# Unread products ahead of ten transpositions of probabilities, and the fourth tile's search rounds at every second unit

## The chip, the cores and the metric

The kernel runs on one core of a Trainium2 chip. The metric is the device time of one execution in microseconds (us). Five engines work side by side, each through its own queue of instructions in order, and wait for one another at semaphores: TensorE (PE in the profile; PEld are its weight loads), VectorE (DVE), ScalarE (ACT), GpSimd (POOL) and SyncE (SP), which only issues transfers.

## The reference, cut to what matters

One transformer layer on 512 rows of width 1024, all in float32. Only the attention part is touched by the change.

```
h = rms_norm(x); proj = h @ w_in              # columns for group A, its indexer, and group B
# group A (8 heads): per query the indexer's score picks 128 keys
score = sum_h relu(qi_h . ki) * wi_h;  idx = top_k(score, 128)
y_a   = softmax(q . k[idx]) @ v[idx]
# group B (4 heads): two maps per head
y_b   = rms_norm((softmax(q1 . k1) - lam * softmax(q2 . k2)) @ v)
x = x + concat(y_a, y_b) @ w_o
x = x + moe(rms_norm(x))                      # 4 of 32 experts per row, dense weights of all 32 read
```

Queries and keys mix causally in chunks of 64 rows.

## The kernel before, in words

The 512 rows are four tiles `t` of 128. The kernel has three parts: the input projection, attention with the output projection and the router, and the experts. The experts' part (`gate_up` and `down`, from about 360 us) streams 384 pieces of weights of 1 MB and splits each into an upper and a lower half.

Up to the experts, the order of all engines is one list, `PLAN`, written by `make_plan` (lines 117 to 218). Each engine walks through the same list and does its own share of each entry, so the list is the order in each engine's queue. Attention is cut into 64 units, numbered by `unit(n)`: a unit is one map of one query tile (`t`, `j`). `j` from 0 to 7 are the eight maps of group B's four heads, `j` from 8 to 15 the eight heads of group A. Units 16 to 23 are group B of tile 0, 24 to 31 group B of tile 1, 32 to 47 tile 2 (B, then A), 48 to 63 tile 3 (B, then A). The function `attend(n)` appends the work of one step, called step n here:

- `score` n: three products into one of two score banks of PSUM (L1704, the mask's product L1706 or L1710, L1711), then the row maximum on VectorE (`nmax`, L1343), then the exponential on ScalarE (L1034).
- `combine`: for group B, after each second unit, VectorE adds the two maps of a head (L1351, L1352, L1355).
- `w_hi` and `w_lo`, in steps 24 to 29 only: a piece of the output weights is rounded by ScalarE (L956) and its remainder taken by VectorE (L552).
- `next_search`: one search round (`topk`) of the indexer's scores. A round finds a row's eight largest values and marks them (MAX8 L1331; value load and MATCH_REPLACE8 L1332). 16 rounds make a tile's mask. Tile 3's rounds 0 and 1 stand in steps 22 and 23, the others from step 32 on.
- `turn_p`: the probabilities of unit n - 2 (group B: of the head that ended with it) are transposed on TensorE (L1651) into one of two transposition banks, `TP_BANK` and the bank after it, and evacuated by ScalarE (L1044).
- `values`: the transposed probabilities of one unit earlier times the values (L1740).
- `LATE`: what stands in a table for step n, among it `mix_b` and `mix_scale` (group B's norm), `turn_y` (transposition of the mixed heads, with a split by L1076 and L1388 or L1391), `out_proj` t k (one of eight parts of tile t's output projection, six products of 512 columns, L1644 to L1646), `post` (x + projection, L1448, and its square on ScalarE, L1095), `turn_x1`, `post_norm` (L1460) and `route` (the router, L1772, and eight small VectorE instructions from L1472 to L1482).

At the start of step 16 t + 7, ahead of its score (step 55 for tile 3), a loop appends all rounds that are left and then `mask` t (L1336), which writes the mask of group A's scores of tile t. The product that adds it in the first such unit (`j` = 8, unit 56 for tile 3) waits for it on TensorE:

```
if t >= 1 and n in (8, 16 * t + 7):
    while search and search[0][1] <= t:
        plan.append(search.pop(0))
    plan.append(("mask", t))
```

`last_unit(pr)` is the number of the last unit of a product `pr` of probabilities and values. `wait_bank` waits until the transposition that used the bank before has been read.

Of the kernel before, what the change touches and what calls it, by code (L numbers as in the profile page):

```python
# [28 lines left out]
P = 128  # L29
SEQ, D = 512, 1024  # L30
T = SEQ // P
# [49 lines left out]
def unit(n):  # L81

    if n < 16:
        return n // 8, 8 + n % 8
    if n < 32:
        return (n - 16) // 8, n % 8
    return n // 16, n % 16
# [6 lines left out]
def product_of(n):  # L94

    if not 0 <= n < UNITS:
        return None
    t, j = unit(n)
    if j < 8:
        return ("B", t, j // 2) if j % 2 else None  # L100
    return ("A", t, j - 8)
# [15 lines left out]
def make_plan():  # L117

    pieces = list(range(4 * (WO + 2)))
    plan = []  # L120
    for k in range(0, KD, 2):
        m = pieces.pop(0)
        plan += [("turn_h", k), ("turn_h", k + 1), ("w_hi", m), ("w_lo", m)]
    plan += [("setup",)]
    scores = [("iscore", t, h) for t in range(1, T) for h in range(HI)]
    search = [("topk", t, r) for t in range(1, T) for r in range(ROUNDS_TOPK)]

    def next_search(n):
        for _ in range(n):
            if search and ("iscore", search[0][1], HI - 1) in plan:  # L130
                plan.append(search.pop(0))

    def lower():

        split = [st[1] for st in plan if st[0] == "w_lo"]
        ready = [st[1] for st in plan if st[0] == "w_hi" and st[1] not in split]
        if plan[-1][0] == "w_hi":
            ready = ready[:-1]
        plan.extend(("w_lo", m) for m in ready[:1])

    def attend(n):
        if n == UNITS + 5:
            plan.append(("biases",))
        if n < UNITS:
            t, j = unit(n)
# [4 lines that stand above are left out]
            plan.append(("score", n))  # L150
        if product_of(n - 1) and product_of(n - 1)[0] == "B":
            plan.append(("combine", product_of(n - 1)))
        if n >= 24:
            if pieces:
                plan.append(("w_hi", pieces.pop(0)))
            lower()
        if n >= 32:
            next_search(1)
        if product_of(n - 2):
            plan.append(("turn_p", product_of(n - 2)))  # L160
        if product_of(n - 3):
            plan.append(("values", product_of(n - 3)))
        plan.extend(LATE.get(n, []))

    attended = list(range(max(LATE) + 1))
    n_items = len(ITEMS)
    first_kv = ITEM_NO[(CH["kvi"], 0)]
    for s in range(n_items + 3):

        def back(d, keep=lambda name: name != "bv"):  # L170

            u = s - d
            return [u] if 0 <= u < n_items and keep(CHUNKS[ITEMS[u][0]][0]) else []

        def all_of(kind, us):
            for u in us:
                plan.append((kind, u))

        def not_bk(name):
            return name not in ("bk", "bv")  # L180

        def only_bk(name):
            return name == "bk"

        fill = ATTEND_AT.get(s, 0)
        all_of("square", back(1))
        for q in range(PARTS):
            if s < n_items:
                plan.append(("proj", s, q))
            if s >= first_kv + 5 and scores and ("turn_heads", first_kv + scores[0][1]) in plan:  # L190
                plan.append(scores.pop(0))
            if q < fill:
                attend(attended.pop(0))
            if q == 0:
                now = []
                while s < n_items and pieces and pieces[0] <= 4 * ITEMS[s][0] + 4 + ITEMS[s][1] \
                        and pieces[0] < 4 * WO:
                    now.append(pieces.pop(0))
                if s < n_items and pieces[0] // 4 == WO and ITEMS[s] == (CH["bv"], pieces[0] % 4 + 1):
                    now.append(pieces.pop(0))  # L200
                all_of("w_hi", now)
                all_of("sums", back(1))
            if q == 1:
                all_of("turn_heads", back(3, not_bk) + back(4, only_bk))
                all_of("heads_hi", back(2, not_bk))
                all_of("w_lo", now)
            if q == 2:
                all_of("heads_hi", back(3, only_bk))
                all_of("norm", back(1))
                all_of("heads_lo", back(2, not_bk))  # L210
            if q == 3:
                all_of("heads_lo", back(3, only_bk))
                all_of("rope", back(1))
            if s < n_items and q < (1 if s < 14 else 3 if s < 18 else 2 if s == 18 else 4):
                next_search(1)
    while attended:
        attend(attended.pop(0))
    return plan
# [5 lines left out]
def number(kinds, count=lambda st: 1):  # L224

    at, out = 0, {}
    for st in PLAN:
        if st[0] in kinds:
            out[st] = at
            at += count(st)  # L230
    out["all"] = at
    return out
# [10 lines left out]
TURN = number(("turn_h", "turn_heads", "turn_p", "turn_y", "turn_x1", "route"), turns_in)  # L243
# [20 lines left out]
def build(nc, x, positions, g_attn, w_in, g_qa, g_ka, g_idx_k, lambda_q1, lambda_k1,  # L264
          lambda_q2, lambda_k2, g_qb, g_kb, g_subln, w_o, g_ffn, w_router, b_router,
          w_gu, b_gu, w_down, b_down, out):
    with ExitStack() as ctx:
        at = {"free": 16512}

        def place(name, shape, dt, offset=None):  # L270

            size = int(np.prod(shape[1:])) * mybir.dt.size(dt)
            size = -(-size // 32) * 32
            if offset is None:
                offset = at["free"]
                at["free"] += size
            return nc.alloc_sbuf_tensor_at(name, shape, dt, offset=offset).ap()
# [78 lines left out]
        identb = place("identb", [P, P], BF16)  # L356
# [40 lines left out]
        ones = place("ones", [P, P], BF16)  # L397
# [14 lines left out]
        ps = ctx.enter_context(nc.psum_tensor("ps", [P, 8, 512], F32))  # L412
        S_BANK, TP_BANK, ACC, OB, OA = 0, 2, 4, 6, 7
# [213 lines left out]
        def tbank(g):  # L627
            return ps[:, TP_BANK + g % 2, :]

        def wait_bank(eng, g):  # L630

            if g >= 2:
                eng.wait_ge(turn_read[g % 2], g // 2)
# [10 lines left out]
        def last_unit(pr):  # L644
            kind, t, h = pr
            return NO[(t, 2 * h + 1 if kind == "B" else 8 + h)]
# [17 lines left out]
        def exp_no(n):  # L664

            return SCORE[("score", n)] + 1

        def combo_no(pr):
            return COMBO[("combine", pr)] + 1
# [264 lines left out]
        def _(act):  # L934
# [9 lines left out]
            for st in PLAN:  # L944
# [117 lines left out]
                elif kind == "mix_scale":  # L1062
# [6 lines left out]
                    ins.then_inc(yb_ok, 1)  # L1069
                elif kind == "turn_y":  # L1070
                    _, t, j = st
                    g = TURN[st]
                    act.wait_ge(turned, g + 1)
# [151 lines left out]
        def _(dve):  # L1225
# [11 lines left out]
            for st in PLAN:  # L1237
# [74 lines left out]
                elif kind == "iscore":  # L1312

                    _, t, h = st
                    v, w = SCORE[st], keys_of(t)
                    dst = work[t]
# [9 lines left out]
                    if h == HI - 1:  # L1326

                        link(dve.memset(work[t][0:CHUNK, w - CHUNK:w], MASKED))
                elif kind == "topk":
                    _, t, r = st  # L1330
                    link(dve.max(top, work[t]))  # L1331
                    link(dve.match_replace(work[t], top, work[t], TAKEN))  # L1332
# [308 lines left out]
        def _(pe):  # L1641
            def three(dst, a, b, k_first, k_last):
# [2 lines left out]
                pe.matmul(dst, a[0], b[1], start=False, stop=False)  # L1645
                return pe.matmul(dst, a[1], b[0], start=False, stop=k_last)  # L1646

            def turn(g, sources):
                wait_bank(pe, g)
                for j, s_ in enumerate(sources):  # L1650
                    ins = pe.transpose(tbank(g)[:, j * P:(j + 1) * P], s_, ident)  # L1651
                ins.then_inc(turned, 1)
# [4 lines left out]
            for st in PLAN:  # L1657
# [3 lines left out]
                elif kind == "proj":  # L1661
                    _, u, part = st
# [13 lines left out]
                elif kind == "turn_heads":  # L1676
                    u = st[1]
                    pe.wait_ge(heads_lo, HEADED.index(u) + 1)
                    for j in range(turns_in(st)):
                        turn(TURN[st] + j, [s_.bitcast(F32) for s_ in turned_heads(u, j)[0]])  # L1680
                elif kind == "iscore":
                    _, t, h = st
# [9 lines left out]
                elif kind == "score":  # L1692
                    n, v = st[1], SCORE[st]
# [17 lines left out]
                    pe.matmul(dst, q, keys[1], start=False, stop=True).then_inc(score_ps, 1)  # L1711
                elif kind == "turn_p":
                    pr = st[1]
                    if pr[0] == "B":
                        pe.wait_ge(combined, combo_no(pr))
                    else:
                        pe.wait_ge(score_read, exp_no(last_unit(pr)))
                    turn(TURN[st], [e_in(pr)[:, rows_of(b)] for b in range(pr[1] + 1)])
                elif kind == "values":
                    pr = st[1]  # L1720
# [21 lines left out]
                elif kind == "turn_y":  # L1742
                    _, t, j = st
                    pe.wait_ge(yb_ok if j else y_ok, t + 1)
                    turn(TURN[st], [y_block(t, 4 * j + k) for k in range(4)])
                elif kind == "out_proj":
                    _, t, i = st
# [17 lines left out]
                elif kind == "route":  # L1765
# [5 lines left out]
                    for k in range(KD):  # L1771
                        ins = pe.matmul(tbank(g)[:, 0:E], x1T[:, k, :], wrt[:, k, :], start=(k == 0),  # L1772
                                        stop=(k == KD - 1))
# [9 lines left out]
            for b in range(T):  # L1783
                ins = pe.matmul(ps[:, TP + 1, T * E:(T + 1) * E], ones, selb[:, b, :], start=(b == 0),
                                stop=(b == T - 1))
# [172 lines left out]
```

## Time and profile before

| what | value |
|---|---|
| time of the runs | 1536.42 us (median of 3; 1532.5 to 1536.57) |
| the profiled execution's own time | 1537.92 us |
| its span, first to last instruction | 1536.0 us |
| TensorE (PE) busy | 1460.7 us, 95% |
| VectorE (DVE) busy | 1310.1 us, 85% |
| ScalarE (ACT) busy | 1105.5 us, 72% |
| GpSimd (POOL) busy | 235.0 us, 15% |
| mean granted TensorE clock | 0.974 |

Busy times are added up over the span, and several engines are busy at once. The granted clock is the share of full speed (1.00 is 2.4 GHz, 0.50 is 1.2 GHz) that TensorE was given. A wait is put down to the instruction that released it.

### The profile page before, as it was taken

What the parts mean: (1) busy time and instruction counts of PE and PEld (TensorE: products, weight loads), DVE (VectorE), ACT (ScalarE), POOL (GpSimd) and SP (SyncE); (2) the same over time, 40 slices, a digit from 0 to 9 for tenths busy, and PEclk for the clock granted to TensorE, in tenths of its full rate; (3) what the DMA queues carried; (4) which work ended last, traced back from release to release, by engine and by line L of the source; (5) the groups of instructions that cost most, each with busy time, mean ns of one, the idle gap of its engine ahead of it and who ended that gap; (6) DMA issues with size and microseconds to landing.
All of it is one profiled execution on the core that took longest, in us unless ns stands there. A gap on an engine that the chain in (4) does not pass through costs nothing.

```text
span 1536.0 us, 18745 instructions
## 1 busy us (share of the span) xinstructions
PE 1460.7 (95%) x7098; PEld 1204.4 (78%) x7098; DVE 1310.1 (85%) x1310; ACT 1105.5 (72%) x1188; POOL 235.0 (15%) x120
## 2 busy tenths in 40 slices
PE   6999878987989999999999999999999999999996
PEld 5887767765778888888888888888888888888885
DVE  5799777547689999999999899999999999989994
ACT  5675554445677788778778887778877877888773
POOL 1222000011111121111121111112111122111101
PEclk9999969997999999999999999999999999999999
DMA  6322011158999999999999999999999999999991
GB/s 185 110 63 62 28 55 42 42 181 331 297 315 356 380 374 369 364 360 369 367 366 376 364 373 365 376 373 371 373 359 362 371 357 374 371 368 362 380 363 29
DMA packets 102316, 448.60 MB, mean 292 GB/s; under 512 B 18496, under 2 KB 23616, under 8 KB 69376
## 3 DMA queue, kind: packets, MB, share of 16 engines
q1 hardware_dynamic: 90336, 428.33, 72.3%
q0 software_dynamic: 9792, 18.90, 5.2%
q8 instruction: 58, 0.95, 0.2%
q10 hardware_dynamic: 2080, 0.01, 0.1%
q14 instruction: 50, 0.41, 0.1%
HBM read 440.89 MB, written 23.07 MB: 302 GB/s over the span
## 4 chain that ended last, share of the span: by engine, by line
PE 88%; DVE 6%; ACT 2%; issue 2%; DMA 1%; POOL 0%; SPq 0%; POOLq 0%; ACTq 0%; DVEq 0%
PE ps L1862 69%; PE ps L1644 2%; PE ps L1645 2%; PE ps L1646 2%; PE ps L1651 2%; PE ps L1872 2%; PE ps L1823 2%; PE ps L1831 2%; PE ps L1740 1%; DVE work L1332 1%; DVE nmax L1343 1%; DVE top L1331 1%; PE ps L1772 1%; PE ps L1711 1%; DMA xs<-in_x_dram 0%
## 5 line engine op out<-in xcount | busy, mean ns | idle before, releaser
L744 DVE TENSOR_TENSOR whl<-wraw,whl 128x2048 fp32r<-128x2048 f32 x384 | 865.9, 2289 | 92.7 <-ACT whl L739 88.5
L739 ACT ACTIVATE whl<-wraw 128x2048 fp32r<-128x2048 f32 x384 | 733.2, 1919 | 207.7 <-PE ps L1862 207.7
L1862 PE MATMUL ps<-whl,xT 128*128 128x512 f32 x3120 | 732.9, 393 | 2.5 <-issue 1.3
L1862 PEld LDWEIGHTS ps<-whl,xT 128*128 128x128 f32 x3120 | 583.1, 189 | 123.6 <-issue 2.4
L1862 PE MATMUL ps<-whl,aT 128*128 128x512 f32 x1488 | 348.2, 393 | 0.0
L1862 PEld LDWEIGHTS ps<-whl,aT 128*128 128x128 f32 x1488 | 278.3, 189 | 57.3
L900 POOL DMA_INDIRECT out_dram<-ysb,idx x32 | 98.1, 3064 | 454.2 <-ACT ysb L1170 440.8
L891 POOL DMA_INDIRECT xg<-h_rows,idx x32 | 89.4, 2795 | 482.0 <-DVE idx L1540 472.4
L1644 PE MATMUL ps<-W,HT 128*128 128x512 f32 (+1 forms) x184 | 72.5, 394 | 1.7 <-DVE HT L1243 1.7
L1645 PE MATMUL ps<-W,HT 128*128 128x512 f32 (+1 forms) x184 | 69.3, 377 | 0.0
L1646 PE MATMUL ps<-W,HT 128*128 128x512 f32 (+1 forms) x184 | 69.1, 375 | 0.0
L1343 DVE TENSOR_REDUCE nmax<-ps 128x1 f32<-128x128 f32 (+3 forms) x64 | 31.3, 488 | 38.7 <-PE ps L1711 37.9
L1034 ACT ACTIVATE raw<-ps,nmax 128x384 f32<-128x384 f32 (+2 forms) x40 | 24.1, 602 | 50.8 <-DVE nmax L1343 50.8
L1162 ACT ACTIVATE acts<-ps 128x1024 f32<-128x1024 f32 x32 | 32.9, 1029 | 26.1 <-PE ps L1862 26.1
L863 POOL TENSOR_TENSOR rstd<-ss,half 128x8 f32<-128x8 f32 (+1 forms) x16 | 26.1, 1630 | 115.1 <-DVE ss L1265 115.1
L1823 PE MATMUL ps<-ident,xg 128*128 128x128 f32 x256 | 35.0, 282 | 8.7 <-DVE gslot L1546 4.4
L1170 ACT ACTIVATE ysb<-ps,gslot 128x1024 f32<-128x1024 f32 x32 | 35.1, 1098 | 10.3 <-PE ps L1862 10.3
L1823 PEld LDWEIGHTS ps<-ident,xg 128*128 128x128 f32 x256 | 31.2, 146 | 13.8 <-issue 5.0
L1552 DVE TENSOR_TENSOR xT<-ps,xT 128x512 fp32r<-128x512 f32 x64 | 41.0, 681 | 0.3 <-ACT xT L1143 0.2
L1644 PEld LDWEIGHTS ps<-W,HT 128*128 128x128 f32 x184 | 35.5, 193 | 6.9 <-DVE HT L1243 2.0
L1143 ACT ACTIVATE xT<-ps 128x512 fp32r<-128x512 f32 x64 | 34.8, 599 | 8.2 <-PE ps L1823 8.2
L1646 PEld LDWEIGHTS ps<-W,HT 128*128 128x128 f32 x184 | 35.4, 192 | 6.7
(243 smaller groups left out, 1371.5 us busy)
## 6 DMA issues: line engine op xcount, KB each, us to landing
wraw<-in_w_gu_dram SPq DMA_DIRECT2D x256, 1024.0 KB, 7.9
wraw<-in_w_down_dram SPq DMA_DIRECT2D x128, 1024.0 KB, 7.5
WR<-in_w_in_dram SPq DMA_DIRECT2D x20, 512.0 KB, 3.7
WR<-in_w_o_dram SPq DMA_DIRECT2D x8, 512.0 KB, 3.7
xs<-in_x_dram SPq DMA_DIRECT2D x4, 512.0 KB, 6.1
WR<-in_x_dram SPq DMA_DIRECT2D x4, 512.0 KB, 3.6
out_dram<-WR SPq DMA_DIRECT2D x4, 512.0 KB, 2.6
h_rows<-WR SPq DMA_DIRECT2D x4, 512.0 KB, 2.6
```

The lines of the kernel that those rows point to most:

```text
L739: act.activation(whl[:, n % HL, 0, :], wraw[n % RAW], ACT.Copy).then_inc(chunk_hi, 1)
L744: eng.tensor_tensor(whl[:, n % HL, 1, :], wraw[n % RAW], whl[:, n % HL, 0, :].bitcast(F32), ALU.subtract).then_inc(chunk_lo, 1)
L891: pool.indirect_dma_start(xg[j % 2], None, hd, bass.IndirectOffsetOnAxis(ap=idx[:, j:j + 1], axis=0), bounds_check=SEQ - 1, oob_is_err=Fal ...
L900: pool.indirect_dma_start(out[0], bass.IndirectOffsetOnAxis(ap=idx[:, e:e + 1], axis=0), ysb, None, bounds_check=SEQ - 1, oob_is_err=False ...
L1170: act.activation(ysb.rearrange("p (a n) -> p a n", a=2), ps[:, dn_bank(e):dn_bank(e) + 2, :], ACT.Copy, scale=gslot[:, e:e + 1]).then_inc( ...
L1343: dve.tensor_reduce(nmax[:, t % 2, j:j + 1], ps[:, S_BANK + v % 2, 0:keys_of(t)], AX.X, ALU.max, negate=True).then_inc(max_ok, 1)
L1552: dve.tensor_tensor(xT[:, 1, 4 * b:4 * b + 4, :], ps[:, TP + b, :].rearrange("p (k n) -> p k n", k=4), xT[:, 0, 4 * b:4 * b + 4, :].bitcas ...
L1644: pe.matmul(dst, a[0], b[0], start=k_first, stop=False)
L1645: pe.matmul(dst, a[0], b[1], start=False, stop=False)
L1646: return pe.matmul(dst, a[1], b[0], start=False, stop=k_last)
L1823: ins = pe.transpose(ps[:, TP + b, k * P:(k + 1) * P], xg[j % 2][:, (4 * b + k) * P:(4 * b + k + 1) * P], ident)
L1862: ins = pe.matmul(bank, a[x_][j], w[:, b, j, 512 * q:512 * q + 512], start=c == NG and j == 0 and n == 0, stop=last and j == nj - 1 and n ...
```

## The change

Two edits.

First, ahead of each `turn_p` whose last unit is from 20 to 39, TensorE waits for the transposition bank and then issues two products of 512 columns (bf16, `identb` against a broadcast of `ones`) into that bank. The transposition overwrites what they leave; nothing reads it. Only group B's products have last units in this range, namely 21, 23 and so on to 39, so there are ten places, in steps 23, 25 and so on to 41, with 20 products in all. They stand ahead of the wait for the probabilities.

Second, from step 32 on a search round is appended only at even steps. Rounds 2 to 15 of tile 3 stood in steps 32 to 45, one each. Now rounds 2 to 13 stand in steps 32, 34 and so on to 54, and rounds 14 and 15 are appended by the loop ahead of `mask` 3, at the start of step 55, behind `post_norm` 1 of step 54 and ahead of score 55. So the odd steps 33 to 45 lose a round each, steps 46, 48, 50, 52 and 54 get one each, and the start of step 55 gets two. In step 52 the round stands ahead of `post` 1.

```
-        if n >= 32:
+        if n >= 32 and n % 2 == 0:
             next_search(1)
...
+            def keep_warm(n, bank=S_BANK):
+
+                for _ in range(n):
+                    pe.matmul(ps[:, bank, :], identb, ones.unsqueeze(1).to_broadcast([P, T, P]), start=True, stop=True)
+
...
                 elif kind == "turn_p":
                     pr = st[1]
+                    if 20 <= last_unit(pr) < 40:
+                        wait_bank(pe, TURN[st])
+                        keep_warm(2, TP_BANK + TURN[st] % 2)
                     if pr[0] == "B":
```

## Rows read from the trace of the kernel before

**Rows 1.** The page, TensorE's granted clock in 40 slices of 38.4 us, in tenths.

```profile
PEclk9999969997999999999999999999999999999999
```

**Rows 2.** Busy time by stretch: us, then engines PE to POOL, granted clock, DMA.

```profile
197.00:200.65 3.65, 1.47 (x11) 1.00 (x11) 3.48 (x12) 1.96 (x7) 0.00 (x0) 1.00 0.02 4
200.65:207.00 6.35, 3.64 (x14) 2.77 (x14) 5.78 (x13) 5.49 (x13) 0.00 (x0) 0.50 0.38 137
207.00:217.70 10.70, 9.45 (x37) 7.71 (x37) 7.79 (x20) 6.64 (x26) 1.01 (x1) 0.50 0.20 66
217.70:221.50 3.80, 2.00 (x12) 1.31 (x11) 2.76 (x6) 2.23 (x6) 0.00 (x0) 0.95 0.00 0
228.00:247.70 19.70, 19.05 (x112) 15.04 (x110) 17.59 (x42) 8.67 (x30) 1.01 (x1) 1.00 0.01 1
247.70:256.00 8.30, 5.03 (x27) 4.11 (x27) 5.68 (x13) 4.74 (x11) 0.55 (x1) 0.79 0.16 63
256.00:279.30 23.30, 23.30 (x144) 19.25 (x143) 11.13 (x27) 10.14 (x33) 2.02 (x1) 1.00 0.13 47
279.30:290.00 10.70, 7.08 (x42) 5.79 (x42) 6.32 (x12) 4.85 (x10) 0.55 (x1) 0.84 0.12 49
296.60:317.00 20.40, 20.40 (x127) 16.75 (x126) 6.70 (x14) 10.07 (x30) 1.01 (x1) 1.00 0.03 12
500.00:1536.00 1036.00, 1022.13 (x4808) 844.46 (x4806) 943.62 (x598) 811.08 (x672) 172.16 (x57) 1.00 0.93 356
```

**Rows 3.** TensorE's waits from 196 to 229 us: total, times, longest.

```profile
PE ps L1740 <- ACT sq L1044: 2.9, 4, 1.6
```

**Rows 4.** TensorE in order of time, `out_proj` 0: start, duration.

```profile
222.67 0.63 PE L1645 MATMUL ps<-W,stk 128*128 128x512 f32 x1
223.10 0.63 PE L1646 MATMUL ps<-W,stk 128*128 128x512 f32 x1
...
228.01 0.39 PE L1645 MATMUL ps<-HT,stk 128*128 128x512 f32 x1
228.24 0.40 PE L1646 MATMUL ps<-HT,stk 128*128 128x512 f32 x1
```

**Rows 5.** All engines in order of time, units 29 and 30.

```profile
209.09 0.42 DVE L1343 TENSOR_REDUCE nmax<-ps 128x1 f32<-128x256 f32 x1 [0.35 <-PE ps L1711]
...
209.58 0.56 PE L1711 MATMUL ps<-W,QB 128*128 128x256 f32 x1
...
210.56 0.42 DVE L1343 TENSOR_REDUCE nmax<-ps 128x1 f32<-128x256 f32 x1
```

**Rows 6.** VectorE's groups of instructions from 214 to 262 us.

```profile
L1331 DVE MAX8 top<-work 128x8 f32<-128x512 f32 x14 | 9.5, 679 | 0.0
L1332 DVE MATCH_REPLACE8 work<-top,work 128x512 f32<-128x512 f32 x14 | 9.5, 676 | 0.0
...
L1332 DVE MATCH_VALUE_LOAD work<-top,work 128x8 f32 x14 | 1.3, 92 | 0.5
```

**Rows 7.** In order of time, behind unit 33's search round.

```profile
221.25 0.75 DVE L1388 SCALAR_TENSOR_TENSOR stk<-ps,gsub,stk 128x512 fp32r<-128x512 f32 x1 [0.27 <-ACT stk L1076]
```

**Rows 8.** In order of time, units 52 and 53.

```profile
279.49 0.69 DVE L1343 TENSOR_REDUCE nmax<-ps 128x1 f32<-128x512 f32 x1 [0.89 <-PE ps L1711]
...
284.90 0.63 PE L1651 MATMUL ps<-ident,WR 128*128 128x128 f32 x4 [2.47 <-ACT sq L1044]
```

**Rows 9.** In order of time, units 55 and 56.

```profile
292.59 0.68 DVE L1343 TENSOR_REDUCE nmax<-ps 128x1 f32<-128x512 f32 x1
...
293.99 0.59 ACT L1044 ACTIVATE sq<-ps 128x512 f32<-128x512 f32 x1
...
294.45 0.25 DVE L1472 SCALAR_TENSOR_TENSOR lg<-ps,tss,brt 128x32 f32<-128x32 f32 x1 [1.17 <-PE ps L1772]
...
296.41 1.05 PE L1740 MATMUL ps<-VB,sq 128*128 128x128 f32 x8
296.61 0.69 DVE L1343 TENSOR_REDUCE nmax<-ps 128x1 f32<-128x512 f32 x1 [0.22 <-PE ps L1711]
```

## The prediction

> **What bounds the kernel.** Times are from the profiled execution: span 1536.0 us, 1537.92 us with what lies around it, 1.5 us above the median of the runs (1536.42). The sum below is of differences against that execution and is then put on the median. Unit n is one query block of one head, and step n is what the order written by hand issues for it. I read the page first, for the clock by slice [rows 1]: two slices are below 9, the sixth (192 to 230 us) at 6, which is the change's, and the tenth at 7, where the experts start. Then the stretches [rows 2]: the expert stage from 500 us on has TensorE 98.7% busy at full clock and none of the change in it, so I take its length as fixed; whatever moves the end of attention moves the end of the kernel by as much. The reader is to see three kinds of stretch in attention. From 200.65 to 217.7 the granted clock is 0.50 (1.2 GHz), and after some full clock it is half again to 228: 512-column products start 0.43 us apart at 222.67 and 0.23 us apart at 228.01 [rows 4]. From 228.0 to 247.7 the clock is full and both TensorE (19.05 of 19.70 us) and VectorE (17.59) are nearly full. From 256.0 to 279.3 and from 296.6 to 317.0 TensorE has no idle time at all and VectorE is half empty. Between them, 279.3 to 290.0, TensorE is idle a third of the time. Then the waits [rows 3] and the order of single instructions.
>
> **The change, part A: 20 unread products.** Ten turn_p steps qualify (last units 21, 23 ... 39), each with two 512-column bf16 products. No such product is in this trace; the nearest are the 512-column fp32r products, which start 0.23 us apart at full clock and 0.43 us apart at half clock [rows 4]. So a pair costs 0.46 us or 0.86 us of TensorE's own queue; the other bound is nothing, where the pair ends inside a wait that is there anyway. I take 0.46 and 0.86 for the queue (same column count) and say below where a wait hides them. All behind a pair in that queue waits for it: the transposition, its evacuation, the next score.
>
> Can they change the clock? In 197.0 to 200.65 TensorE was busy 1.47 of 3.65 us and the clock fell; in 207.0 to 217.7 it was busy 9.45 of 10.70 us and the clock rose at the end; in 217.7 to 221.5 it was busy 2.00 of 3.80 and the clock fell again [rows 2]. Before the first fall, units 24 to 26 pass with just one pair among them (ahead of last unit 23's transposition), so I expect the first fall to stay. From unit 27 on every second unit has a pair; at half clock these fill much of the waits of the values products (2.9 us in four, the longest 1.6 [rows 3]), so I expect the rise earlier, near 211, and no second fall, as the pair of last unit 31 lands in the pause at 217.8.
>
> The Trainium skill (TensorE: Matmul & The Clock Gate, Why this matters for your kernels) says that the clock is lost by long pauses of the engine between bursts. The rows do not agree: no pause from 196 to 229 is over 1.6 us [rows 3], and the clock fell twice. By that rule such short pauses would cost no clock and the products could win nothing; that result is the rival R1 below, priced from rows.
>
> What a full clock is worth: little up to unit 33, because the order there is set by ScalarE and VectorE, which split the output weights between the units' work. VectorE waits for TensorE only 0.35 us before the row maximum of unit 29; the maximum of unit 30 comes 0.4 us after its last product ends (209.58 + 0.56), because a split is in between [rows 5]. Fully warm, units 29 to 33 come 0.44 us earlier; with the fall kept and pairs at 0.86 us, unit 30's maximum comes 0.45 us later (its last product ends at 210.14 + 0.86 = 211.0, and its maximum was at 210.56). Then out_proj 0: of the twelve products of its first two parts, from 222.1 to 228.5, about eleven run at 0.43 instead of 0.23 us [rows 4]: 2.2 us, plus 0.5 us for the scores and transpositions between, less the pair of 0.46 us: 2.25 us. That is the gain at unit 36: 2.25 + 0.44 = 2.7 us fully warm, 2.25 - 0.45 = 1.8 us as I expect it.
>
> Against this, steps 37, 39 and 41 have pairs at full clock in a stretch that is full: 3 x 0.46 = 1.4 us. About 0.9 us of it replaces idle time there (19.70 - 19.05 = 0.65, and what the removed rounds free, below). So 0.5 us is lost. **Part A: -1.3 us.**
>
> **Part B: the rounds that leave.** Seven rounds go from units 33, 35 ... 45. A round is MAX8 0.68, value load 0.09 and MATCH_REPLACE8 0.68 us [rows 6], 1.45 us. That is 10.2 us of VectorE, nearly all under cover. At unit 33 VectorE has idled 0.27 us behind the round before the next instruction starts at 221.25, when ScalarE's evacuation ends [rows 7]: nothing. Unit 35: 0.35 us, counted above. Units 37 and 39: VectorE runs 0.4 us ahead, which serves the pairs' cost. Unit 41: the maximum of unit 42 waits for TensorE anyway. Unit 43: the split of y waits for ScalarE. Unit 45: TensorE is full. If I am wrong and VectorE leads throughout 228 to 248, the bound is TensorE's idle time there, 0.65 us, and that of 247.7 to 256.0 (8.30 - 5.03 = 3.3 us) [rows 2], 3.9 us in all. **Part B: 0.**
>
> **Part C: where they arrive.** Units 46 and 48: TensorE is full and VectorE half empty (256.0 to 279.3), cost 0. Unit 50: the maximum of unit 51 is 0.6 us late, absorbed by the 0.89 us of idle ahead of the maximum of unit 52. Unit 52: the round stands ahead of `post` 1. From that maximum (279.49) VectorE runs without a pause through the combination and x1 to the maximum of unit 53; ScalarE squares x1, takes unit 53's exponential and evacuates, and TensorE waits 2.47 us for it [rows 8]. All of it shifts: +1.5 us. Three more rounds come ahead of the maximum of unit 55: one in step 54 behind the combination, two behind `post_norm` 1 and ahead of `mask` 3. Mask 3 stood right ahead of the maximum of unit 55 at 292.59, which becomes 292.59 + 1.5 + 3 x 1.45 = 298.4. Behind that maximum stand route 1's small instructions (294.45 to 0.22 us before 296.61, 1.95 us), then the maximum of unit 56: 298.4 + 0.65 + 1.95 = 301.0 against 296.61, +4.4 us. On TensorE score 56 waits for the mask, and the values of (B,3,2) wait for unit 55's exponential and the evacuation (whose start was 1.4 us behind the maximum, 0.59 us long): 298.4 + 1.4 + 0.6 + 0.2 = 300.6 against 296.41 [rows 9], +4.2 us. Behind it TensorE is full until 317, so nothing takes it back. The bounds: 1.5 us if the two final rounds found cover, 6 us if all of unit 55's delay (5.85) came through. **Part C: +4.2 us.** The wait is new: TensorE's score 56 on the mask (about 1.1 us), behind it everything of attention.
>
> The new pauses near 283 and 298 may also stretch the half clock that the stretch 279.3 to 290.0 already holds (mean 0.84, so 10.70 x 0.16 x 2 = 3.4 us of it); as much again would cost half of it, 1.7 us. I leave it to the range.
>
> **Sum:** -1.3 + 0 + 4.2 = +2.9 us, 1536.42 + 2.9 = 1539.3 us. A measurement tells 0.3%, 4.6 us, from nothing; the forecast is no measurable change, leaning slow.
>
> **Rivals.**
> R1, the clock does not follow: the pairs cost 0.86 us each at half clock and win nothing. Unit 32's maximum 1.2 us late, 0.86 more at unit 35, about 0.5 net in the full stretch: +2.5, with C +6.7: 1543.1. For: in 200.65 to 207.0 TensorE is busy only 3.64 of 6.35. Against: it rose unaided at 217.7. With the further half clock 1544.8.
> R2, slower by C alone (the side opposite to a gain): A as forecast, but both delays of C (1.5 at unit 52, 5.9 at unit 55) reach the end, with 1.7 us of clock: -1.3 + 5.9 + 1.7 = +6.3: 1542.7. It decides if TensorE finds nothing to do between score 56 and those values and each later unit waits for its own evacuation; the walk above lets it recover 1.7 us.
> R3, fully warm from 197 on: -2.2 + 4.2 = +2.0: 1538.4. Against: the thin units 24 to 26.
> R4, the late rounds find cover and only unit 52's 1.5 counts: -2.2 + 1.5 = -0.7, or to -4.6 with B's bound of 3.9: 1531.8 to 1535.7. Against: the maximum of unit 55 has the three rounds ahead of it in VectorE's own queue, and the maximum of unit 56 had 0.22 us of slack [rows 9].
> R5, the change does not do what it says: the pairs run wholly inside waits and rounds move under cover, no effect: 1536.4. Against: [rows 9] again.
>
> **Chances.** Forecast 0.42, R1 0.17, R2 0.11, R3 0.13, R4 0.10, R5 0.07. Slower by over 0.3% (above 1541.0): R1, R2: 0.28. Faster by over 0.3% (below 1531.8): only R4's far end touches it: 0.03. The rest 0.69. Range 1534.6 to 1543.4: it leaves out the far ends of R4 and of R1. The forecast's own: 1537 to 1541.
>
> **What would show it.** A: the clock by stretch, 0.50 from about 200 to about 211 and full from there through 228; score 36 about 2 us nearer to score 24. B: VectorE idle in 228 to 248 and TensorE no less busy. C: the maxima of units 54 to 56: 54 late by 1.5, 55 by about 6, 56 by about 4.4 against unit 52; a TensorE wait on mask 3. Wrong if TensorE has no pause around mask 3, if the clock stays half to 217, or if the expert stage's length moves by more than 1 us (its own low-clock stretches at the start can fall otherwise).

## The result, and the profile after

The changed kernel takes 1541.71 us (median of 12 runs, 1540.02 to 1542.8) against 1536.49 us for the kernel before (12 runs, 1532.5 to 1539.68) on the same chip. The medians are 5.2 us apart. The recorded ratio is an estimate from the single executions and not the quotient of the medians: 1.0038, with a 95% interval of 1.0028 to 1.0047, or 5.8 us slower, from 4.3 to 7.2 us. The forecast was 1539.3 us, +2.9, no measurable change. The measured time lies inside the range that it gave (1534.6 to 1543.4), but outside of the forecast's own band (1537 to 1541) and past its bound of 0.3%, on the slow side: the range holds it because it was drawn wide enough for the rivals R1 and R2. Of all executions in this document one was in a slow state, with rounds only (2450.84 us at a granted clock of 0.558), and it is left out of that kernel's ratio.

The profiled execution has a span of 1540.9 us against 1536.0. The same view as [rows 2], by the stretches of this trace (us, then TensorE, its weight loads, VectorE, ScalarE and GpSimd, granted clock, DMA):

```profile
195.00:202.16 7.16, 4.14 (x27) 2.76 (x26) 6.42 (x19) 5.27 (x14) 0.00 (x0) 1.00 0.01 5
202.16:209.00 6.84, 5.36 (x21) 3.95 (x19) 6.34 (x10) 4.67 (x11) 0.00 (x0) 0.50 0.41 151
209.00:219.20 10.20, 5.90 (x37) 3.98 (x37) 5.78 (x17) 5.97 (x25) 1.01 (x1) 1.00 0.17 52
219.20:226.00 6.80, 6.49 (x19) 4.66 (x20) 4.04 (x9) 1.99 (x6) 0.00 (x0) 0.50 0.00 0
226.00:247.00 21.00, 20.88 (x122) 16.21 (x120) 13.51 (x33) 9.16 (x31) 1.01 (x1) 1.00 0.00 1
247.00:256.00 9.00, 6.02 (x26) 5.00 (x26) 4.81 (x10) 5.38 (x14) 0.55 (x1) 0.66 0.14 58
279.30:287.50 8.20, 3.89 (x26) 2.77 (x25) 5.41 (x11) 4.43 (x12) 0.00 (x0) 1.00 0.16 65
287.50:294.30 6.80, 6.14 (x23) 5.47 (x24) 4.92 (x11) 1.93 (x4) 0.55 (x1) 0.50 0.00 0
505.00:1540.90 1035.90, 1021.98 (x4807) 844.30 (x4805) 943.39 (x598) 810.22 (x672) 173.01 (x57) 1.00 0.93 356
```

The last line is the experts: 1035.9 us with TensorE busy 1021.98, as before (1036.0 and 1022.13). So the whole difference between these two traces arose ahead of them. The clock lines are to be read against [rows 2]. Before, half clock ran from 200.65 to 217.7 and again from 221.1 to 228.0. Now it is half from 202.16 to 209.0 and full from there to 219.2, with TensorE busier at half clock (5.36 of 6.84 us). Then it is half again to 226.0, and in that stretch lies the first part of the output projection. From 226 to 247 TensorE is busy 20.88 of 21.00 us, and VectorE has dropped to 13.51.

To see where time goes I take the start of every unit's row maximum (L1343), which exists in all the kernels. Starts are counted from the maximum of unit 24, because the traces reach it at different times (before at 199.41, after at 197.69, all kernels between 196.66 and 199.78), while of the change only the first of the ten pairs lies ahead of it. The table has each start less that of the kernel before. A positive number is late, in us.

| unit | before, start | after | products only | rounds only |
|---|---|---|---|---|
| 29 | 209.09 | -0.01 | 0.00 | -0.01 |
| 30 | 210.56 | +0.42 | +0.40 | 0.00 |
| 34 | 221.92 | +0.35 | +0.40 | -0.08 |
| 36 | 229.22 | +0.49 | +0.58 | -1.81 |
| 42 | 244.73 | +1.03 | +1.19 | -2.13 |
| 48 | 268.47 | +2.10 | +2.26 | -1.08 |
| 52 | 279.49 | +2.09 | +2.26 | -1.08 |
| 54 | 289.34 | +3.61 | +2.12 | +0.44 |
| 55 | 292.59 | +8.17 | +2.36 | +4.99 |
| 56 | 296.61 | +6.58 | +2.62 | +3.41 |
| 63 | 317.77 | +6.52 | +2.63 | +3.33 |

The column "after" has three steps: 2.1 us grow between units 29 and 48 (0.4 at unit 30, 0.5 between units 36 and 42, 1.1 between 42 and 48), 1.5 us come at unit 53 and 3.0 us at unit 56, after a peak at unit 55.

The first number of these is plain in the instructions (start, duration; in brackets the idle time ahead and what ended it). The unread pair and the transposition behind it, unit 29's maximum, the last product of unit 30's score, unit 30's maximum:

```profile
207.13 1.08 PE L1651 MATMUL ps<-ones,identb 128*128 128x512 bf16 x2
207.36 0.42 DVE L1343 TENSOR_REDUCE nmax<-ps 128x1 f32<-128x256 f32 x1 [0.35 <-PE ps L1716]
...
208.00 0.63 PE L1656 MATMUL ps<-ident,raw 128*128 128x128 f32 x2
...
208.74 0.48 PE L1716 MATMUL ps<-W,QB 128*128 128x256 f32 x1
...
209.26 0.42 DVE L1343 TENSOR_REDUCE nmax<-ps 128x1 f32<-128x256 f32 x1 [0.34 <-PE ps L1716]
```

At half clock the pair takes 208.00 - 207.13 = 0.87 us of TensorE's queue. Against [rows 5], VectorE now waits for the product that stands behind it. (In the changed kernel L1651 is the unread pair; what was L1651, L1711 and L1740 is L1656, L1716 and L1748.) Next, TensorE's pause ahead of `turn_y` 0 1, in the kernel before:

```profile
219.27 0.63 PE L1651 MATMUL ps<-ident,WR 128*128 128x128 f32 x4 [1.47 <-DVE stk L1391]
```

And in the changed kernel:

```profile
214.60 0.60 PE L1651 MATMUL ps<-ones,identb 128*128 128x512 bf16 x2
215.04 0.38 PE L1656 MATMUL ps<-ident,raw 128*128 128x128 f32 x2
...
217.97 0.63 PE L1656 MATMUL ps<-ident,WR 128*128 128x128 f32 x4 [2.55 <-DVE stk L1391]
```

The pair takes 0.44 us at full clock, yet the pause that follows the transposition behind it is 2.55 us, where it was 1.47. At full clock TensorE had finished its own work earlier and only waited longer for VectorE. Behind that pause come `out_proj` 0's products (the view of [rows 4]):

```profile
222.58 0.63 PE L1645 MATMUL ps<-HT,stk 128*128 128x512 f32 x1
223.00 0.63 PE L1646 MATMUL ps<-HT,stk 128*128 128x512 f32 x1
...
227.10 0.39 PE L1646 MATMUL ps<-HT,stk 128*128 128x512 f32 x1
```

222.58 and 223.00 are 0.42 us apart, at half clock as before; full clock is back at 226. The gain that was forecast for this place is absent.

Units 53 to 56, the places of [rows 8] and [rows 9]. First the maximum of unit 53 and TensorE's wait:

```profile
284.23 0.68 DVE L1343 TENSOR_REDUCE nmax<-ps 128x1 f32<-128x512 f32 x1
...
286.80 0.63 PE L1656 MATMUL ps<-ident,WR 128*128 128x128 f32 x4 [3.98 <-ACT sq L1044]
```

The wait was 2.47 us and is 3.98: 1.5 us longer, one round. Then the end of the search, mask 3 (L1336), the maximum of unit 55, score 56, the values of (B,3,2) and the maximum of unit 56:

```profile
295.67 0.68 DVE L1331 MAX8 top<-work 128x8 f32<-128x512 f32 x1
...
298.69 0.43 DVE L1336 TENSOR_SCALAR maskA<-work 128x512 bf16<-128x512 f32 x1
...
299.04 0.68 DVE L1343 TENSOR_REDUCE nmax<-ps 128x1 f32<-128x512 f32 x1
299.06 0.40 PE L1709 MATMUL ps<-KAI,QA 128*128 128x512 f32 x1
...
301.07 1.16 PE L1748 MATMUL ps<-VB,sq 128*128 128x128 f32 x8 [1.16 <-ACT sq L1044]
...
301.47 0.68 DVE L1343 TENSOR_REDUCE nmax<-ps 128x1 f32<-128x512 f32 x1
```

The maximum of unit 55 starts right behind the mask. Score 56's first product starts at 299.06, right behind `out_proj`'s last product, so TensorE has no pause ahead of the mask; it was itself late, at half clock until 294.3. It waits 1.16 us at the values.

### The profile page after: what moved, and what is told of

Its sections match the earlier page's. It is cut to its first block, busy times and chain, and to the rows that moved or that the text cites. A ratio compares the mean times of both kernels' runs of the same rounds, so it can differ in the third digit from the quotient of the medians.

```text
span 1540.9 us, 18783 instructions
## 1 busy us (share of the span) xinstructions
PE 1462.9 (95%) x7118; PEld 1203.7 (78%) x7118; DVE 1310.5 (85%) x1310; ACT 1104.8 (72%) x1188; POOL 235.8 (15%) x120
## 4 chain that ended last, share of the span: by engine, by line
PE 87%; DVE 7%; ACT 3%; issue 2%; DMA 1%; POOL 0%; SPq 0%; POOLq 0%; ACTq 0%; DVEq 0%
PE ps L1870 68%; PE ps L1644 2%; PE ps L1646 2%; PE ps L1645 2%; PE ps L1656 2%; PE ps L1880 2%; PE ps L1831 2%; PE ps L1839 2%; PE ps L1748 1%; DVE work L1332 1%; DVE nmax L1343 1%; DVE top L1331 1%; DMA h_rows<-WR 0%; PE ps L1716 0%; DMA xs<-in_x_dram 0%
## 5 line engine op out<-in xcount | busy, mean ns | idle before, releaser
L1343 DVE TENSOR_REDUCE nmax<-ps 128x1 f32<-128x128 f32 (+3 forms) x64 | 31.1, 488 | 40.2 <-PE ps L1716 39.4
```

The lines of the kernel that those rows point to most:

```text
L1343: dve.tensor_reduce(nmax[:, t % 2, j:j + 1], ps[:, S_BANK + v % 2, 0:keys_of(t)], AX.X, ALU.max, negate=True).then_inc(max_ok, 1)
```

## Experiments

Each kernel was run in 12 executions beside the kernel before (29 to 35 executions, medians 1534.36 to 1535.78 us). Ratios are to those, as above, and a difference given with a ratio is worked out from it. From each kernel there is one trace.

**Each half of the change alone.** The first kernel has the `turn_p` edit and `if n >= 32:`; the second has

```
-        if n >= 32:
+        if n >= 32 and n % 2 == 0:
             next_search(1)
```

and no products. Expected of the first:

> The 20 unread products alone; the search rounds stand in steps 32 to 45 as before. Theory A (the trace of after: the pairs raise the clock early, it falls again ahead of out_proj 0, and four pairs lie in the full stretch): +1.5 to +2.5 us against before. Rival (the forecast's part A, clock kept through out_proj 0): -1.3 us. Rival 2 (all of the slowdown comes from the products): +5 to +6 us.

Of the second:

> The rounds at even steps alone, no products. Theory A (unit 52's round 1.5 us, the three ahead of unit 55's maximum some 3 us more): +4.0 to +4.7 us against before, and the maximum of unit 55 about 5.9 us late, that of unit 56 about 4.4. Rival (the late rounds are under cover and the products make the slowdown): -1 to +1 us.

Measured: products only 1537.8 us, ratio 1.0021 (1.0005 to 1.0037), +3.2 us (the medians are 2.1 us apart); rounds only 1540.7 us, 1.0032 (1.0018 to 1.0046), +4.9 us. Both cost. The column of the products ends at +2.63 us and shows a gain nowhere: the forecast's part A had the wrong sign. With the rounds alone, 4.4 us come between units 52 and 63 (-1.08 to +3.33), as in "after" (+2.09 to +6.52). Its earlier -1.8 us at unit 36 is not the rounds' own: in that execution the half clock between units 24 and 36 was 17.1 us in all instead of 23.9, and three later orders with the same steps 32 to 42 show -0.2, 0.0 and -1.4 there. The products' clock (stretches with the same columns as above):

```profile
209.00:219.20 10.20, 5.99 (x38) 4.09 (x37) 6.59 (x21) 5.99 (x24) 1.01 (x1) 1.00 0.17 52
219.20:226.00 6.80, 6.32 (x19) 4.49 (x20) 5.24 (x12) 2.04 (x6) 0.00 (x0) 0.51 0.00 0
226.00:247.00 21.00, 20.81 (x121) 16.23 (x121) 18.04 (x44) 9.22 (x32) 1.01 (x1) 1.00 0.01 1
```

Full, half, full, as in the changed kernel: full clock did come early and was lost at the same place.

The step between units 42 and 48 (1.1 us in "after", products only and rounds only alike) is neither half's own. It goes with the length of the half clock near 250, here of the rounds alone:

```profile
247.00:256.00 9.00, 8.52 (x41) 6.93 (x40) 5.29 (x10) 3.74 (x13) 1.59 (x2) 0.64 0.01 3
```

It lasts 6.8 us in these three traces and 3.4 us in the kernel before, behind a pause of the same length (2.44 to 2.45 us). What decides between the two lengths is not shown.

**The rounds thinned, but not late.** No products. Even steps to 42, then one each at steps 44 to 51:

```
-        if n >= 32:
+        if n >= 32 and (n % 2 == 0 or n >= 44):
             next_search(1)
```

> No products. Rounds at even steps from 32 to 42, then one at each step from 44 to 51, so odd steps 33 to 43 are as free as in the change and nothing stands in steps 52 to 55. Theory A: leaving the odd steps wins 0 to 0.5 us and the arrival costs nothing: -0.5 to +0.5 us. Rival (thinning the odd steps itself costs or wins): outside of this by more than 1 us.

1536.09 us, ratio 1.0004 (0.9989 to 1.0019), unit 63 at +0.52. Emptying the odd steps wins nothing that can be told from zero (-0.5 us at unit 43 in the trace), and rounds up to step 51 cost little; part B's zero stands.

**One round at step 52; two at step 55.** The same order, with the round of step 51 in step 52 (`and n != 51`), and with those of steps 50 and 51 at the start of step 55 (`and n < 50`).

> No products. The thinned order that ended at step 51, with its last round in step 52 instead, ahead of post 1. Theory A: the maxima of units 53 and 54 another 1.5 us later than with that order, +1.5 us against it, +1.7 to +2.1 against before. Rival (one round is absorbed): 0 to +0.7 us.

> No products. The thinned order with its last two rounds (those of steps 50 and 51) at the start of step 55, ahead of mask 3; none in steps 50 to 54. Theory A: unit 55's maximum 2.9 us late, of which unit 56's and TensorE's values keep 1.3 to 2.7 us because TensorE has the router and out_proj 2 1 to do meanwhile; +1.3 to +2.9 us against before. Rival (covered by that work): 0 to +0.7 us.

1536.37 us, 1.0009 (0.9993 to 1.0025), and 1537.14 us, 1.0008 (0.9995 to 1.0021): by time neither is told from no change. The maxima tell more. With the one round, unit 52 is at -0.09 and unit 53 at +1.43: the 1.5 us. A further 1.2 us come to unit 56 (+2.65) while the half clock that begins near 286 lasts 6.8 us where the kernel before had 3.4. With the two, unit 54 is at -2.11 (a lead that the trace has since unit 48, ahead of where the order differs), unit 55 at +0.93 and unit 56 at -0.65: 3.0 us late at the mask, of which 1.5 us remain. So, by the traces, the changed kernel's 4.4 us are 1.5 us from the round at step 52 and 3.0 us from the three ahead of mask 3 (4.5 us of VectorE's queue, of which TensorE's router, `out_proj` 2 1 and a wait's slack cover a third).

**Where the products cost.** The rounds as before the change, and pairs only for last units 21 to 31, none in the full stretch:

```
-                    if 20 <= last_unit(pr) < 40:
+                    if 20 <= last_unit(pr) < 32:
```

> No change of the rounds. Pairs only ahead of the transpositions of last units 21 to 31 (steps 23 to 33), none in steps 35 to 41. Theory A (the loss of the products is mostly the four pairs in TensorE's full stretch and what follows from them): 0 to +0.8 us against before, unit 30's maximum 0.4 us late and units 41 to 50 within 0.7 us. Rival (the pairs' harm is done before unit 34): +2 to +3 us, as with all 20 products.

1535.36 us, 1.0001 (0.9988 to 1.0014). Unit 30 is at +0.50, unit 36 at -1.31, units 41 to 50 at -1.32 to -0.39 (expected within 0.7), unit 63 at -0.21. No loss shows without the four pairs of steps 35 to 41, though the interval overlaps that of all 20 products. In the traces the two end 2.8 us apart. Of this, 0.6 us come between units 36 and 43, where the three pairs at full clock are: that is their price. 1.9 us come at units 35 and 36, where only the pair of step 35 differs and the half clock from 221 lasted 3.4 us instead of 6.8. Whether that pair or chance made it longer is not shown.

**The pause filled.** As the last, with eight products instead of two in step 33:

```
-                        keep_warm(2, TP_BANK + TURN[st] % 2)
+                        keep_warm(8 if last_unit(pr) == 31 else 2, TP_BANK + TURN[st] % 2)
```

> As the kernel before with pairs in steps 23 to 31, and eight products instead of two in step 33, ahead of TensorE's pause before out_proj 0. Theory A (the forecast's gain was missed only because the clock fell again in that pause): the clock stays full through out_proj 0, unit 36's maximum 1.5 to 2.3 us earlier than in the variant with two, -1 to -2 us against before. Rival (more products only cost queue time): +0.5 to +2 us.

1535.69 us, 1.0002 (0.9990 to 1.0014). The stretches:

```profile
211.30:221.00 9.70, 6.83 (x42) 4.47 (x42) 6.42 (x19) 5.63 (x23) 1.01 (x1) 1.00 0.18 55
221.00:227.90 6.90, 5.71 (x31) 4.32 (x31) 6.42 (x15) 2.60 (x8) 0.00 (x0) 1.00 0.00 0
...
248.90:256.00 7.10, 6.62 (x27) 5.32 (x26) 4.11 (x8) 3.61 (x14) 0.55 (x1) 0.52 0.01 2
```

The clock is full through `out_proj` 0 (221.0 to 227.9), and unit 36 is at -1.89, near the -1.8 that the forecast had for it. (That figure of the forecast has the pair of step 35 taken off, which this order lacks.) It is 2.4 us ahead of the changed kernel's (+0.49), of which the missing pair is 0.46 to 0.86 us; against the last kernel (-1.31, with 3.4 us of half clock from 221.0) it is 0.6 us, less than the 1.5 to 2.3 expected. Part of it is lost near 250 (0.52 from 248.9 to 256.0), as in the last kernel, where the pause of step 33 is not filled: unit 48 is at -0.82, and unit 63 at -0.41. By time nothing can be told from zero.

**The rounds taken off the chain.** No products. The 14 rounds at steps 33 to 41, 43 and 46 to 49:

```
-        if n >= 32:
+        if n >= 33 and n not in (42, 44, 45):
             next_search(1)
```

> No products. The same 14 rounds at steps 33 to 41, 43 and 46 to 49; none in steps 32, 42, 44, 45 or after 49. Theory A (a round costs only where VectorE's queue is the chain: step 32 ahead of mix_scale 0, step 42 ahead of post 0): 1.4 us won at each, -2 to -3 us against before. Rival (the chain there is ScalarE's or TensorE's): -0.5 to +0.5 us.

1529.75 us against 1535.74, ratio 0.9964 (0.9947 to 0.9980): 5.5 us faster, more than expected. VectorE's step of `mix_scale` 0 (L1370), ScalarE's behind it, and TensorE's `turn_y` 0 1 (before: 1.5 us of waiting there):

```profile
212.35 0.11 DVE L1370 TENSOR_TENSOR rl<-rl,rstd 128x4 f32<-128x4 f32 x1
...
212.50 1.14 ACT L1067 ACTIVATE WR<-ps,rl 128x128 f32<-128x128 f32 x4 [0.31 <-DVE rl L1370]
...
215.26 0.87 PE L1651 MATMUL ps<-ident,WR 128*128 128x128 f32 x4 [0.20 <-DVE stk L1391]
```

The pause of TensorE has shrunk to 0.20 us. Unit 33 is at -1.26, one round; unit 35 at -2.39 and unit 36 at -3.63, where the trace has full clock (from 215.8 on) and the kernel before had half; unit 43 at -4.77 and unit 46 at -6.35, where the trace has no half clock near 250; unit 63 at -6.06.

**The faster order with products.** With the pairs to unit 31 and eight products in step 33; with five more in step 43; and with all 20 products of the change:

> The rounds at steps 33 to 41, 43 and 46 to 49 (the faster order), with pairs in steps 23 to 31 and eight products in step 33. Theory A (a gain of clock at out_proj 0 is partly given back at the pause of step 43): 0 to -1 us against that order without products, so -5.5 to -7 against before. Rival (the products only cost): +0.5 to +1 against that order.

> The same, with five products more in step 43 ahead of the transposition of unit 41, before TensorE's pause at turn_y 1 1. Theory A (that pause is what takes the clock next): no half clock near 250, another -0.5 to -1.5 us. Rival (they delay the transposition and what follows): +0.3 to +1 us.

> The faster order of the rounds with all 20 products of the change. Theory A (the four pairs of steps 35 to 41 cost 1.4 to 1.9 us of TensorE's full stretch whatever the rounds do): -3 to -4.5 us against before, 1.5 to 2.5 slower than the order without products. Rival (with VectorE relieved they are hidden): -5.5 to -6.5 us.

1530.75 us (0.9976, 0.9961 to 0.9991), 1530.24 us (0.9972, 0.9960 to 0.9985) and 1534.51 us (1.0000, 0.9986 to 1.0013). The first two beat the kernel before but do not improve on the order without products, against the 0 to 1 us that the first was expected to win over it. Their traces have unit 63 at -4.04 and -4.57 against -6.06. The second is the expected 0.5 us ahead of the first, but no more. The first has 3.4 us of half clock from 247.1, which the order without products does not have, and falls 1.6 us behind that order between units 43 and 46. In the second that half clock is gone, as expected, and one from 279 is 6.8 us long instead of 3.4. The third is worse than expected: by time the products take back all that the order won. Its profiled execution shows 2.7 us of that (unit 63 at -3.39 against -6.06); the rest was not seen in it.

## Why the prediction was right or wrong, point by point

**Bound.** Right for these two traces: the expert stage kept its length to 0.1 us, and attention's end moved the kernel's. It is no fixed length, though. In the thirteen traces of this document the time from unit 63's maximum to the end is 1213.5 to 1219.5 us (before 1218.2, after 1218.3), with the same instructions in it.

**Part A, -1.3 us forecast, +2.1 us in the trace (+2.6 alone; by time +2.1 between the medians, +3.2 by the ratio).** Its pieces:
- A pair's price, 0.46 and 0.86 us: right, 0.44 and 0.87. Unit 30's maximum came 0.42 us late, forecast 0.45. The sentence that no such product is in the trace of before was wrong: the mask's product of tile 3 (L1710) is one, 512 columns in bf16, eight times.
- The first fall stays and the clock rises near 211: right, 209.0.
- "No second fall": this is the step that failed. The forecast put the pair of last unit 31 into the pause at 217.8. It does run ahead of the pause, but at full clock TensorE finishes sooner while the thing that it waits for (mix_scale 0 through ScalarE to VectorE's L1391) keeps its time. The pause grew from 1.47 to 2.55 us and the clock fell at 219.2. The gain of 2.25 us at `out_proj` 0 was lost with it. Eight products there kept the clock and put unit 36 at -1.89 us, where the forecast had -1.8: the size was about right (the forecast's is for one pair more, at 0.46 us) and the condition wrong.
- The pairs in the full stretch: forecast 0.5 us net, since 0.9 of their 1.4 us would replace idle time. Right: from unit 36 to unit 42 the changed kernel lost 0.54 us and products alone 0.61.
- The half clock near 250: the forecast has no term for it. It lasted 6.8 us instead of 3.4, and the changed kernel lost another 1.1 us between units 42 and 48. The experiment without pairs in this stretch lost 0.9 us there and the rounds alone, with no product at all, 1.05 us, so this is not the pairs' queue time. Why it was longer is open; in a part of the traces it may be chance.

The forecast's first rival (the clock brings nothing, +2.5 for the products) is nearest to what happened in part A, though for another reason than it gave: the clock did follow and was lost again. That its total (1543.1 us, as R2's 1542.7) is nearer to the measured time than the forecast's is in part luck: it adds queue time that the traces show only in part, and leaves out the half clock near 250. The Trainium skill's rule about long pauses (TensorE: Matmul & The Clock Gate, Why this matters for your kernels) speaks of longer pauses than any that stands ahead of the two falls here. It comes nearer to the second, which followed a pause of 2.55 us, than to the first, where no wait ahead of it was over 1.71 us.

**Part B, 0 us.** Right as far as time can tell: the thinned order that isn't late took 1.0004 of the time before, with +0.5 us at unit 63 in the trace.

**Part C, +4.2 us.** Right: 4.4 us in both traces. Unit 51's maximum came 0.6 us late and unit 52's did not, as forecast, unit 52's round cost 1.5 us, unit 55's maximum moved by 8.17 - 2.09 = 6.1 us (forecast 5.85) and unit 56's by 4.5 (forecast 4.4). One detail was wrong, and it is one that the forecast had named as a sign of being wrong: TensorE does not wait for mask 3. It was late itself, through 6.8 us of half clock instead of 3.4 (the 1.7 us that the forecast left to the range). The cost of that ran beside VectorE's delay and did not add to it: VectorE works without a pause from the maximum of unit 54 to that of unit 56. The forecast put the further half clock down to the longer pause at 283. That is not shown: the order with two rounds at step 55 has 6.8 us of it too, behind a pause of 2.46 us, as long as before. That VectorE's queue carries the delay was right.

**Sum.** 2.1 + 4.4 = 6.5 us in the trace. The span grew by 4.9 only, because the profiled execution of the changed kernel was 1.7 us ahead at unit 24, a difference that lies ahead of nearly all of the change. By time it is 5.2 us between the medians and 5.8 by the ratio. Against the forecast's +2.9, part A is 3.4 us off: 2.3 at unit 36, where the gain of `out_proj` 0 is missing, and 1.1 behind unit 42, at the half clock near 250.

Open: why the 20 products on the faster order cost more by time (about 5 us against that order alone, compared across two measurements; 3.8 us against the first kernel of the last three, in one measurement) than up to unit 63 in the traces (2.7 and 0.7 us). For the products alone there is no such gap: 2.1 us between the medians, 3.2 by the ratio, 2.6 in the trace. The executions of one kernel range over 9 us, and a trace is one of them.

## What to carry to other kernels

Price a moved instruction by who stands behind it in its engine's own queue at the new place: three search rounds ahead of one mask cost twice what one round did at a place where all of VectorE's queue was the chain, and nothing where TensorE was full. Filler that brings the full clock early does not keep it by itself: a pause that another engine sets gets longer when TensorE gets faster (here from 1.47 to 2.55 us). Two products ahead of it did not keep the clock; eight did, and by time nothing was left of it. So take what lengthens the pause off that engine's queue first, which here won 5.5 us with no filler at all. In a stretch where TensorE is nearly full, filler is cost: 0.6 us for three pairs.

## What the runs showed of the hardware that was not expected

Half clock taken away is not time won in the same measure. Between the maxima of units 24 and 63 the kernel before has 30.7 us of half clock, the changed kernel 27.3, the pairs to unit 31 20.5 and the filled pause 17.1; the last two take as long as the kernel before by time. The faster order has 20.5 us of it without products and 13.7 with each of the three sets of products, and is fastest in its trace without them.

The same half clock comes in two lengths. The one near 250, behind a pause of 2.45 us, lasts 3.4 us in the kernel before, in the order thinned but not late and in the two orders made from it, and 6.8 us in the changed kernel, with either half alone, with pairs to unit 31 and with the pause of step 33 filled. With the pause of step 43 filled it is gone, and the one near 279 lasts 6.8 us instead of 3.4: the same total as with that pause left open.

Executions of the unchanged kernel on one chip spread from 1530.1 to 1539.5 us. Traces differ by up to 3.1 us at unit 24, where only the first pair of the change lies ahead, among other things by whether a short half clock near 166 is there, and by up to 6.0 us between unit 63's maximum and the end, where the instructions are the same. So gains of 1 to 2 us at one place of one trace say little about the median.
